# Decoder block on one core: branch weights split inside attention's last head, tiles laid out by slot, the last store's wait moved, the attention branch first in the mixing stage

## The reference

```python
attn = mla_attention(c_q, c_kv, k_rope_raw, cos, sin, g_cq[l], w_uq[l], g_ckv[l], w_ukv[l])
conv = gated_short_conv(bcx, conv_w[l])
g_a, g_b = jnp.split(gates, N_BRANCHES, axis=-1)
mixed = g_a * (attn @ w_branch_a[l]) + g_b * (conv @ w_branch_b[l])
x = x + mixed @ w_out[l]
```

## Time and profile before

| | |
|---|---|
| median of 3 executions | 2878.9 us (2871.32 to 2881.54) |
| the profiled execution's own time | 2871.8 us |
| its span, first to last instruction | 2870.0 us |
| mean granted TensorE clock | 0.964 of full speed |
| attention's last value product ends | 1379.5 us from the span's start |
| first matmul of mixing | 1390.9 us |
| first output product of mixing | 1424.9 us |

### The profile page before, as it was taken

The page is one execution under the profiler, slowest core; times in us unless marked ns, Lnnn a source line. Parts: engine busy times, 40 slices in busy tenths (PEclk is TensorE's granted clock), DMA queues, the critical chain, the costliest instruction groups (busy, mean ns, idle before and its releaser), DMA issues. The chain is left out here.

```text
span 2870.0 us, 38196 instructions
## 1 busy us (share of the span) xinstructions
PE 2651.3 (92%) x12854; PEld 2085.2 (73%) x12854; DVE 1668.3 (58%) x2334; ACT 1390.1 (48%) x2316; POOL 671.8 (23%) x708
## 2 busy tenths in 40 slices
PE   6999999999998999999799999899958999999980
PEld 5777777787785777777699987677646777777760
DVE  3623624523524676776554444566567888888858
ACT  4334334333324776776411113543417777777753
POOL 0000000000003665664322220000003444444430
PEclk9999999999998999999899999999979999999995
DMA  4253353354442122112444436132268999999978
GB/s 169 85 182 134 99 181 122 115 173 176 127 145 58 40 55 52 41 37 83 134 139 121 144 107 214 30 110 96 93 256 296 375 372 375 372 385 387 373 280 358
DMA packets 168851, 508.67 MB, mean 177 GB/s; under 512 B 40448, under 2 KB 69760, under 8 KB 140576
## 3 DMA queue, kind: packets, MB, share of 16 engines
q1 hardware_dynamic: 150016, 472.56, 47.8%
q0 software_dynamic: 18720, 34.64, 3.2%
HBM read 432.21 MB, written 108.33 MB: 188 GB/s over the span
## 5 line engine op out<-in xcount | busy, mean ns | idle before, releaser
L494 DVE TENSOR_TENSOR fr_wl<-fr_raw,fr_wh 128x1024 fp32r<-128x1024 f32 x128 | 156.8, 1225 | 469.9 <-ACT fr_wh L365 469.6
L365 ACT CAST fr_wh<-fr_raw 128x1024 fp32r<-128x1024 f32 x128 | 134.0, 1047 | 493.3 <-PE fr_acc L282 258.6
L2578 DVE TENSOR_TENSOR ex_gl<-ba_raw,ex_gh 128x2048 fp32r<-128x2048 f32 x128 | 293.2, 2292 | 104.0 <-ACT ex_gh L2491 104.0
L974 DVE TENSOR_REDUCE at_nm<-at_psA 128x1 f32<-128x512 f32 (+2 forms) x320 | 191.4, 608 | 142.5 <-PE at_psA L858 82.6
L2491 ACT CAST ex_gh<-ba_raw 128x2048 fp32r<-128x2048 f32 x128 | 245.2, 1917 | 38.8 <-PEq L2086 38.8
L1058 POOL TENSOR_TENSOR at_pl<-at_pf,at_ph 128x512 fp32r<-128x512 f32 (+1 forms) x160 | 191.3, 1195 | 215.7 <-ACT at_ph L941 215.3
L2428 PE MATMUL ex_psG<-ex_gh,ex_xh 128*128 128x512 f32 x512 | 200.7, 392 | 6.7 <-DVE ex_xl L2583 5.3
L1034 POOL CAST at_vh<-all_cst 128x32 fp32r<-128x32 f32 x2 | 0.5, 228 | 854.2 <-POOLq L111 854.2
L2429 PE MATMUL ex_psG<-ex_gl,ex_xh 128*128 128x512 f32 x512 | 200.2, 391 | 0.0
L2430 PE MATMUL ex_psG<-ex_gh,ex_xl 128*128 128x512 f32 x512 | 200.2, 391 | 0.0
L940 ACT ACTIVATE at_pf<-at_psS 128x512 f32<-128x512 f32 (+3 forms) x240 | 125.2, 522 | 80.7 <-PE at_psS L824 41.9
(11 more groups left out here) (403 smaller groups left out, 6702.3 us busy)
## 6 DMA issues: line engine op xcount, KB each, us to landing
ba_raw<-in_w_exp SPq DMA_DIRECT2D x192, 1024.0 KB
fr_raw<-in_w_slabs SPq DMA_DIRECT2D x128, 512.0 KB, 3.8
gates_d<-fr_gst SPq DMA_DIRECT2D x64, 256.0 KB, 4.3
mx_gt<-gates_d SPq DMA_DIRECT2D x64, 256.0 KB, 5.2
cb_ys<-y_d SPq DMA_DIRECT2D x16, 1024.0 KB, 11.6
mx_xr<-in_x SPq DMA_DIRECT2D x8, 1024.0 KB, 7.1
x_d<-mx_xo SPq DMA_DIRECT2D x8, 1024.0 KB, 5.0
xa_xe<-x_d SPq DMA_DIRECT2D x16, 512.0 KB, 5.1
```

The lines of the kernel that those rows point to most:

```text
L365: nc.scalar.copy(wh[:, i % 2], raw[:, i % 2]).then_inc(w_hi, 1)
L494: V.tensor_tensor(wl[:, i % 2], raw[:, i % 2], wh[:, i % 2], ALU.subtract).then_inc(w_lo, 1)
L974: V.tensor_reduce(nm[:, i, c:c + 1], psA[b][:, 0:w], AX, ALU.max, negate=True).then_inc(a_max, 1)
L2578: V.tensor_tensor(gl[:, s, i], raw[:, r, i, :].rearrange("p (k n) -> p k n", k=KD // 2), gh[:, s, i], ALU.subtract).then_inc(w_lo, 1)
```

## The change

- The operands of attention are no longer one tile with two slots, but a tile for each slot, all of slot 0 first. The output staging `ost` moves ahead of them, and the branch weights' split tiles `wap` and `wbp` are laid over slot 0 (`wap` wholly, `wbp` but for its last 4 KB), so that they can be written in the last head.
- In the last head ScalarE makes the four high parts of `w_branch_a` after tiles 11, 13, 15 and 17, waiting for both weights' loads. VectorE makes the four low parts in steps 17 to 20, the division three to four steps earlier than before (reciprocals in 21, 23, 25, 27, the product in 28), then high and low parts of `w_branch_b` in steps 29, 31, 33 and 35, but the last low part, which stays in `mix`. ScalarE's and GpSimd's split of the divided rows moves from steps 34 and 36 to 30 and 32.
- The wait for the last stores moves from attention's end into the first chunk of `mix`, ahead of the next chunk's loads. `w_branch_a` is loaded first.
- `mix` starts with ScalarE's copy of the convolution's rows and the copies of `w_out`; VectorE does the one low part that is left and the low part of the convolution's rows of the first chunk, which was GpSimd's.
- In every chunk the attention's piece comes before the convolution's; in the first chunk the order is attention 0, attention 1, convolution 0, convolution 1, and then in turn.
- `gb` of the cross-attention takes the place that `ost` has used.

```diff
@@ attention, scalar
-                    if not more and u == 34:
+                    if not more and u in (11, 13, 15, 17):
+                        k = (u - 11) // 2
+                        if k == 0:
+                            act.wait_ge(pv, NU * h + PR)
+                            act.wait_ge(mixer["ab_in"], 32)
+                        nc.scalar.copy(wap[:, 0, k, :], wa_raw[:, k, :]).then_inc(mixer["w_hi"], 1)
+                    if not more and u == 30:
@@ attention, vector
-                    if not more and u in (24, 26, 28, 30):
...
+            def last_head(u):
+                if u in (17, 18, 19, 20):
+                    k = u - 17
+                    dve.wait_ge(mixer["w_hi"], k + 1)
+                    V.tensor_tensor(wap[:, 1, k, :], wa_raw[:, k, :], wap[:, 0, k, :], ALU.subtract).then_inc(mixer["w_lo"], 1)
+                if u in (21, 23, 25, 27):
+                    f = (u - 21) // 2
+                    dve.wait_ge(mixer["ar_in"], 48)
+                    V.reciprocal(lr[:, f, :], lr[:, f, :]).then_inc(mixer["inverted"], 1)
+                if u == 28:
+                    dve.wait_ge(mixer["inverted"], 4)
+                    V.tensor_tensor(ar[:], ar[:], lr[:], ALU.mult).then_inc(mixer["divided"], 1)
+                if u in (29, 31, 33, 35):
+                    k = (u - 29) // 2
+                    V.tensor_copy(wbp[:, 0, k, :], wb_raw[:, k, :]).then_inc(mixer["wb_hi"], 1)
+                    if k < 3:
+                        dve.wait_ge(mixer["wb_hi"], k + 1)
+                        V.tensor_tensor(wbp[:, 1, k, :], wb_raw[:, k, :], wbp[:, 0, k, :], ALU.subtract).then_inc(mixer["w_lo"], 1)
@@ attention, gpsimd
-                    if not more and u == 36:
+                    if not more and u == 32:
                         pool.wait_ge(mixer["in_hi"], 1)
@@ attention, sync
-            for b in range(2):
-                sp.wait_ge(o_st[b], 32 * (2 * H + 1))
@@ mix, sync
                     xrows(0)
+                    for b in range(2):
+                        sp.wait_ge(mixer[f"o_st{b}"], 32 * (2 * H + 1))
@@ mix, tensor
+                order = list(range(2 * KD))
+                if first:
+                    order[1], order[2] = 2, 1
...
-                            pe.wait_ge((c_lo, a_lo)[a], c + 1)
+                        pe.wait_ge((a_lo, c_lo)[a], c + 1)
@@ mix, scalar
-            for i in range(4):
-                high(i)
             conv_high(0)
-            for i in range(4, 8):
-                high(i)
             for i in range(8, 12):
                 high(i)
@@ mix, vector
-            for i in range(8):
-                low(i)
+            low(7)
+            dve.wait_ge(in_hi, 2)
+            V.tensor_tensor(cT[:, 1], cv[:], cT[:, 0], ALU.subtract).then_inc(c_lo, 1)
```

More of the change, by code:

```diff
@@ L688, in attention @@
         vraw = s_.sb("vraw", [P, NT, VD])
[L689 to L694, removed]
+        qh, ql, kh, kl, vh, vl = ([], [], [], [], [], [])
+        for e in range(2):
+            for n, tiles, shape in (("qh", qh, [KA, T]), ("ql", ql, [QKD, T]), ("kh", kh, [KA, T]), ("kl", kl, [QKD, T]),
+                                    ("vh", vh, [P, NT, VA]), ("vl", vl, [P, NT, VA])):
+                tiles.append(s_.sb(f"{n}{e}", shape, F32R))
+            if e == 0:
+                assert nc.sbuf_base >= held_at + 60 * D
         pf = s_.sb("pf", [P, PR, CH])
@@ L820, in scores @@
                 pe.wait_ge(hi, NU * h + u + 1)
-                nc.tensor.matmul(out, kh[:, s, k], qh[:, s, q], start=True, stop=False)
-                nc.tensor.matmul(out, kh[0:QKD, s, k], ql[:, s, q], start=False, stop=False)
+                nc.tensor.matmul(out, kh[s][:, k], qh[s][:, q], start=True, stop=False)
+                nc.tensor.matmul(out, kh[s][0:QKD, k], ql[s][:, q], start=False, stop=False)
                 diag = j >= 4 * c
-                mm = nc.tensor.matmul(out, kl[:, s, k], qh[0:QKD, s, q], start=False, stop=not diag)
+                mm = nc.tensor.matmul(out, kl[s][:, k], qh[s][0:QKD, q], start=False, stop=not diag)
                 if diag:
@@ L839, in products @@
                 r = u % PR
-                nc.tensor.matmul(out, vh[:, s, j, :], ph[:, r, off:CH], start=(j == 0), stop=False)
-                nc.tensor.matmul(out, vh[:, s, j, :], pl[:, r, off:CH], start=False, stop=False)
-                nc.tensor.matmul(out, vl[:, s, j, :], ph[:, r, off:CH], start=False, stop=last).then_inc(pv, 1)
+                nc.tensor.matmul(out, vh[s][:, j, :], ph[:, r, off:CH], start=(j == 0), stop=False)
+                nc.tensor.matmul(out, vh[s][:, j, :], pl[:, r, off:CH], start=False, stop=False)
+                nc.tensor.matmul(out, vl[s][:, j, :], ph[:, r, off:CH], start=False, stop=last).then_inc(pv, 1)
             def maxima(h, s, v):
@@ L857, in maxima @@
                 diag = c == i // 4
-                mm = nc.tensor.matmul(psA[b][:, 0:w], qh[0:QKD, s, i * P:(i + 1) * P], kh[0:QKD, s, c * CH:c * CH + w], start=True, stop=not diag)
+                mm = nc.tensor.matmul(psA[b][:, 0:w], qh[s][0:QKD, i * P:(i + 1) * P], kh[s][0:QKD, c * CH:c * CH + w], start=True, stop=not diag)
                 if diag:
@@ L1017, in head @@
                             top(h + 1, v)
-                    if not more and u in (24, 26, 28, 30):
-                        f = (u - 24) // 2
-                        dve.wait_ge(mixer["ar_in"], 48)
-                        V.reciprocal(lr[:, f, :], lr[:, f, :]).then_inc(mixer["inverted"], 1)
-                    if not more and u == 32:
-                        dve.wait_ge(mixer["inverted"], 4)
-                        V.tensor_tensor(ar[:], ar[:], lr[:], ALU.mult).then_inc(mixer["divided"], 1)
+                    if not more:
+                        last_head(u)
+            def last_head(u):
[16 more added lines that the diff above has]
+                        V.tensor_tensor(wbp[:, 1, k, :], wb_raw[:, k, :], wbp[:, 0, k, :], ALU.subtract).then_inc(mixer["w_lo"], 1)
             heads(dve, head)
```

99 lines of the change are left out of this document (49 added, 50 removed).

## The result

| | before | after |
|---|---|---|
| median of 12 executions each, us | 2875.7 (2871.32 to 2881.54) | 2882.1 (2877.09 to 2888.28) |
| the profiled execution, us | 2871.8 | 2879.9 |
| its span, us | 2870.0 | 2878.0 |
| mean granted TensorE clock | 0.964 | 0.967 |

The ratio of after to before is 1.0023, with a 95% interval of 1.0014 to 1.0032: the change costs 6.6 us (4.0 to 9.2). That is slower, and inside the 0.5% that the prediction called no change. The forecast was +8.2 us and 2887 us.

A forecast was written before the change was run, and what follows sets the result against it. TensorE, busy 92%, was taken as the bound, with mixing's first chunk ending on gates queued behind w_out loads. Terms 11.4 - 6.6 + 3.4 = +8.2 us on 2871.8 gave 2880, or 2887 on the median; range 2871 to 2896.

The forecast's parts named there:

- partial-exclusion rival: Last head: more GpSimd work hidden under reciprocals or copies, part 4 at 5 to 9, 2881 to 2885 us; chance 0.20.
- part 4: Last head: VectorE's added weight work is serial with GpSimd's and delays attention's end, ScalarE's load wait included; +11.4 us.
- 24.9 + 14.5 - 3.6 = 35.8: Last head, us: VectorE's own work plus GpSimd's, less the GpSimd work hidden under reciprocals.
- The copies: Last head: VectorE's four 1024-column copies, some 0.65 us each, 2.6 in all, taken as serial with GpSimd's work.
- third rival: Last head: ScalarE's wait for the divided rows feeds back, TensorE idles into the lower clock; about 2895 us; chance 0.10.
- Parts 1 and 2: Attention's end and mixing's first chunk: earlier block start without the stores' wait, and earlier low(11) and gates; -6.6 us.
- Part 3: Start of chunk 1, attention's piece first: gap no longer filled, +1.4, and lower clock behind it, +2.0; together +3.4 us.
- The +1.4 of the order: Start of chunk 1: the convolution's piece of 1.44 us no longer fills TensorE's wait for the split rows; +1.4 us.

The follow-up runs named there:

- experiments 1 and 2: 1: changed kernel with VectorE's last-head weight work back in mixing, ratio 0.9995; 2: the same, plus unread one-input maxima on VectorE in its place, ratio 1.0004.
- experiment 5: Changed kernel, but in the first chunk the gates of blocks 4 to 7 are issued each ahead of its w_out piece; ratio 1.0007.
- experiment 6: Changed kernel with the convolution's piece first again in chunks 1 to 7; ratio 1.0020.

## Why the prediction was right, and where its terms were off

The verdict (slower, within 0.5%) and the sign were right, and so was the mechanism of the loss. The sum was near: +8.2 forecast, +5.9 in the trace, +6.6 in the medians. But 2882.1 us lies below the forecast's own 2884 to 2890, in the numbers of the partial-exclusion rival (2881 to 2885), whose condition, part 4 at 5 to 9, did not hold. Of the 4.9 us between 2887 and 2882.1, 3.2 are the base: the median of three executions of before was 2878.9, that of twelve is 2875.7.

- **Part 4, +11.4: measured +11.1.** The mechanism was shown by experiments 1 and 2 together. The steps inside it were less exact than the sum, and that two errors cancelled is luck. VectorE's stretch began 14.5 us behind tile 11 (forecast 14.8). The serial time of VectorE and GpSimd, my 24.9 + 14.5 - 3.6 = 35.8, was 34.2 (1350.59 to 1384.80). From there to the end of the last product it was 3.0 us, not 1.4: that is the lower clock behind the gap of 2.98 us, which I had named only as a bound. At the higher clock, as in experiment 5, part 4 is +9.6. ScalarE's wait was forecast at 5.4 us behind tile 11 and was 5.22, and TensorE's stall for it was 0.77 instead of 1.4; taking it away is worth 3.4 us of the last head in one execution against one, where I gave 1.8. Whether the two effects add can't be told: without VectorE's weight work there are 8.7 us less, without ScalarE's wait 3.4, together 12.1 of 11.1, and the difference is within the scatter.
- **The copies.** My price was 0.65 us, the row has 0.69. Beside GpSimd it is 1.77 (1378.41, GpSimd at work from 1377.90 to 1382.97), so copies do take turns with GpSimd's work. By the rule of the Trainium skill (SBUF — State Buffer, "Who interferes with whom") it should be so, and the trace agrees with it: 0.69 against 1.77. No run separates what this makes of the head's time.
- **The feedback of the third rival** was there, small: ScalarE waited 3.08 us for the divided rows and GpSimd 4.80 for ScalarE. It did not pass the point from which it decides (part 4 above 17.6).
- **Parts 1 and 2, -6.6: measured -6.0.** `low(11)` ends 6.5 us earlier against the copy, the stores' wait is worth 1.3 us at the first matmul. Two more executions of the same first chunk give -4.7 and -4.9 instead of -6.0. The rest of the difference is TensorE's piece behind the gates: it waited 4.05 us and took 2.93 and 2.50 for two pieces, where before it had 2.36, 2.62 and 2.22. That TensorE's early start is worth nothing by itself is shown by 1, where it starts 4.6 us later and the output comes 0.6 later; that the chain runs through the gates, by 5.
- **Part 3, +3.4: measured +0.9. This term was mis-sized.** I had taken the gap at 2.1 us and, as "nearer to 2.36", the lower clock behind it at +2.0. The gap was 1.46 and the pieces behind it took 1.69 and 1.60: the clock stayed at 2.4 GHz. Over the changed kernels the gap at this place and the first piece behind it were 0.71 and 1.69, 0.90 and 1.70, 1.37 and 1.69, 1.68 and 1.69, 1.71 and 1.69, 1.74 and 1.69, 2.15 and 1.70, 2.22 and 1.69, but 1.95 and 2.74, 3.72 and 2.92. The length of a gap does not decide by itself; I had made it do so from one row. The other end of my range for this term, 0, was the right one in nine of the eleven. The +1.4 of the order fits the 1.2 us between the kernels of either order (experiment 6), but no pair of kernels at the same clock isolates it.

## What to carry to other kernels

Before moving work to an engine that looks idle, ask what it shares with its neighbour. VectorE's subtractions and float32 copies took turns with GpSimd's subtractions, and cost their own time on both; maxima over SBUF and reciprocals ran beside them at full speed. And before taking work out of a stage, find the chain that ends it: 11 us of VectorE's weight work, hidden behind a chain of gates, was worth 0.6 us there, which is within the scatter. When the gates were issued earlier, the four low parts of `wap` alone (4.9 us of it) became worth 2.2. Where both hold, spread the work over steps with a gap behind each: four low parts in a row cost 3.5 us, the same four some five steps apart, in a head with less waiting, nothing that could be seen. And count a lower clock behind a stall as a chance, not as a term: here it came behind some gaps of 2 to 3 us and not behind others.

## What the runs showed of the hardware

The clock that TensorE is granted behind the same gap differs between executions. The last heads of after and of experiment 5 are the same code: behind 2.98 us the products went to 0.63 us each (1.2 GHz), behind 2.99 us they stayed at 0.39, and that was worth 1.4 us.

The same is seen at the start of cross-attention, whose first matmul comes behind an idle time of 2.90 us in before and in after. Timeline of TensorE before:

```profile
1771.26 0.77 PE L1637 MATMUL xa_psQ<-all_hh,all_wqh 128*128 128x512 f32 x1 [2.90 <-DVEq L1988]
```

and after:

```profile
1774.39 0.47 PE L1659 MATMUL xa_psQ<-all_hh,all_wqh 128*128 128x512 f32 x1 [2.90 <-DVEq L2010]
```

Before, the clock granted from 1773 to 1777 is 0.50, the level of 1.2 GHz; after, from 1776 to 1780, it is 1.00. All eleven kernels with the change have the higher level here, so that one execution of before does not show whether this is chance or comes with the change. Nor was the higher clock worth anything here: ScalarE waited 7.93 us for the load of `w_o_mem` where it had waited 4.08 before, TensorE then waited 5.10 us for ScalarE instead of 1.26, and after lost 2.7 us in this stretch. Here TensorE was not what the stage waited for, so its lower clock in before cost nothing that can be seen. This scatter of single executions is why the medians, not the two profiled executions (8.1 us apart), give the cost of the change.
